# The second block's mixer in the order conv, q, k, pool, v, with its side work spread over the units

## The reference

```python
h = rms_norm(x, mix_norm[l])
u = h @ w_in[l]                       # 1024 -> conv 512, pool 256, q 512, k 512, v 512
y_conv = conformer_conv(...)          # a * sigmoid(gate), 31 taps over the tokens, layer norm, silu
y_pool = multiscale_pool(...)         # windows of 2, 4, 8, 16 tokens, then a 64 x 64 product per group
q = rms_norm(q.reshape(..., 4, 2, 64), q_norm[l]) * 64 ** -0.5
k = rms_norm(k.reshape(..., 4, 2, 64), k_norm[l])
...
a = p[:, :, 0] - lam * p[:, :, 1]     # p: softmax of q k^T - slope * distance, two maps per head
o = einsum(a, v)
y_attn = rms_norm(o, attn_subln[l]) * (1 - lambda_init)
x = x + concatenate([y_conv, y_pool, y_attn]) @ w_out[l]
```

## Time and profile before

| | |
|---|---|
| median of 3 runs | 2148.89 us (2148.51 to 2149.14) |
| the profiled execution | 2149.96 us, span 2148.1 us |
| PE busy in the span | 2097.4 us (98%) |
| DVE, ACT, POOL busy | 1253.8, 1091.8, 112.6 us |
| the two stages that the change touches | 1349.8 to 1463.9 us, 1838.0 to 1953.6 us |

### The profile page before, as it was taken

How to read it: one execution, slowest core, us unless ns; L and a number is a source line. 1 busy time by engine, 2 the same in 40 slices (tenths; PEclk the granted TensorE clock), 3 DMA queues, 4 the chain that set the end, 5 groups by cost and what they waited for, 6 DMA issues and landing times.

```text
span 2148.1 us, 24565 instructions
## 1 busy us (share of the span) xinstructions
PE 2097.4 (98%) x9840; PEld 1730.9 (81%) x9840; DVE 1253.8 (58%) x1609; ACT 1091.8 (51%) x1554; POOL 112.6 (5%) x128
## 2 busy tenths in 40 slices
PE   7999999999999999999999999979999999979998
PEld 6888788888888887888888888868888888868886
DVE  5555666555655556665556555676555555675554
ACT  5444564544554455554446444675444444665443
POOL 1000100000000000000000000140000000140000
PEclk9999999999999999999999999989999999989999
DMA  6554635555555554455556555525554655515553
GB/s 230 194 185 162 207 125 200 177 187 185 187 191 177 194 168 147 157 181 187 186 190 224 188 193 185 171 69 175 187 190 163 224 182 185 181 65 174 179 184 120
DMA packets 104545, 379.04 MB, mean 176 GB/s; under 512 B 11745, under 2 KB 11905, under 8 KB 104176
## 3 DMA queue, kind: packets, MB, share of 16 engines
q1 hardware_dynamic: 101808, 368.23, 51.6%
q0 software_dynamic: 2080, 8.21, 1.1%
q10 hardware_dynamic: 544, 1.05, 0.2%
HBM read 374.82 MB, written 2.62 MB: 176 GB/s over the span
## 4 chain that ended last, share of the span: by engine, by line
PE 86%; issue 9%; DVE 3%; ACT 2%; DMA 0%; POOL 0%; DVEq 0%; POOLq 0%; ACTq 0%
PE pb L333 26%; PE pb L335 26%; PE pb L334 25%; DVE scr L1297 2%; PE pb L389 2%; PE pb L352 1%; PE pb L375 1%; PE pb L427 1%; PE pb L373 1%; PE pb L374 1%; DVE wlo L1287 1%; ACT scr L1142 1%; PE pb L526 0%; ACT whi L866 0%; PE pb L500 0%
## 5 line engine op out<-in xcount | busy, mean ns | idle before, releaser
L1287 DVE TENSOR_TENSOR wlo<-raw,whi 128x1024 fp32r<-128x1024 f32 (+1 forms) x704 | 839.4, 1219 | 316.3 <-ACT whi L866 312.3
L866 ACT ACTIVATE whi<-raw 128x1024 fp32r<-128x1024 f32 (+1 forms) x704 | 716.3, 1050 | 212.3 <-PE pb L335 202.9
L333 PE MATMUL pb<-whi,XTh 128*128 128x512 f32 (+2 forms) x1904 | 751.3, 395 | 4.4 <-DVE wlo L1287 4.4
L335 PE MATMUL pb<-whi,XTl 128*128 128x512 f32 (+2 forms) x1904 | 737.6, 387 | 0.0
L334 PE MATMUL pb<-wlo,XTh 128*128 128x512 f32 (+2 forms) x1904 | 736.6, 387 | 0.0
L333 PEld LDWEIGHTS pb<-whi,XTh 128*128 128x128 f32 x1904 | 359.5, 189 | 79.6 <-DVE wlo L1287 5.9
L335 PEld LDWEIGHTS pb<-whi,XTl 128*128 128x128 f32 x1904 | 359.0, 189 | 74.3
L334 PEld LDWEIGHTS pb<-wlo,XTh 128*128 128x128 f32 x1904 | 359.7, 189 | 68.2
L333 PE MATMUL pb<-whi,HTh 128*128 128x512 f32 x816 | 321.5, 394 | 8.5 <-DVE HTl L1297 8.5
L335 PE MATMUL pb<-whi,HTl 128*128 128x512 f32 x816 | 319.2, 391 | 0.0
L334 PE MATMUL pb<-wlo,HTh 128*128 128x512 f32 x816 | 319.0, 391 | 0.0
(11 more groups left out here) (209 smaller groups left out, 1117.7 us busy)
## 6 DMA issues: line engine op xcount, KB each, us to landing
raw<-in_W SPq DMA_DIRECT2D x696, 512.0 KB, 4.2
raw<-in_W SPq DMA_DIRECT2D x8, 264.0 KB, 2.7
scratch<-scr POOLq DMA_DIRECT2D x1, 1536.0 KB, 6.4
scr<-in_bc POOLq DMA_DIRECT2D x2, 640.0 KB, 5.4
X<-in_x ACTq DMA_DIRECT2D x2, 512.0 KB, 9.1
scr<-scratch POOLq DMA_DIRECT2D x1, 1024.0 KB, 7.0
scr<-in_slope POOLq DMA_DIRECT2D x1, 1024.0 KB, 9.3
scr<-in_Pg POOLq DMA_DIRECT2D x1, 1024.0 KB, 12.5
```

The costliest lines, as they stand in the source:

```text
L333: pe.matmul(o, ah, bh, start=begin and i == 0, stop=False)
L335: ins = pe.matmul(o, al, bh, start=False, stop=end and done)
L866: return act.activation(o, i, ACT.Copy, scale=scale)
L1287: dve.tensor_tensor(wlo[u % W_SLOTS][:, 0:c], raw[u % RAW_SLOTS][:, 0:c], whi[u % W_SLOTS][:, 0:c].bitcast(F32), ALU.subtract).then_inc(*u ...
```

## The change

The 18 units of the input projection come in the order conv (k = 0 to 3), q (4 to 7), k (8 to 11), pool (12, 13), v (14 to 17), and the host lays the weights out so. The output projection takes its chunks as pool (2, 3), conv (0, 1), attention (4 to 7). The taps go by two lists, some at each k from 6 to 18, on ACT and DVE; POOL does the additions of taps 1 to 5, the root of q, taps 6 to 16, the root of k, taps 17 to 30. The batches that stood ahead of unit 18 on PE are spread over k = 15 to 22. The mean and variance of the conv norm come from `bn_stats` and `bn_aggr` on DVE, straight from PSUM, and DVE applies them, in place of two passes with sums and one to apply on ACT. `POOL_TAPS` is empty. In the core of the diff the lines that were removed from the loops are left out, since they stand in the functions above; the order of the hunks is PE, ACT, DVE, POOL, host.

```diff
-OUT2 = [2, 3, 4, 5, 6, 7, 0, 1]
+OUT2 = [2, 3, 0, 1, 4, 5, 6, 7]
...
+ACT_TAPS = [0, 3, 6, 9, 12, 15, 17, 19, 21, 23, 24, 26, 28, 31]
+DVE_TAPS = [0, 3, 6, 8, 11, 13, 16, 18, 21, 23, 25, 27, 29, 31]
...
+POOL_TAPS = range(31, 31)
+POOL_AT = (6, 17)
...
                     if k == 1:
                         rest(n)
...
+                    if k == 6:
+                        turn_pair(z, ("z", i, 1), "z", 4, ("zp", i))
+                    if k == 11:
+                        turn_head(q2, "q", 0, 5)
+                        turn_head(q2, "q", 1, 6)
                     if k == 15:
...
+                        turn_head(k2, "k", 0, 7)
+                        turn_head(k2, "k", 1, 4)
+                        pooled(0, 5)
+                        logits(0, 0, (6, 2))
+                        logits(0, 2, (3, 7))
+                        pooled(2, 4)
+                    if k == 16:
+                        pool_groups(4)
+                        logits(1, 0, (5, 6))
                     if k == 17:
...
+                        turn_pair(y[:, :, 256:512], ("pool_y", i), "pool", 7, ("pool_l", i, 1))
+                        logits(1, 2, (4, 3))
                     if k == 18:
...
+                        turn_maps(0, 0, 5)
+                        turn_maps(0, 2, 6)
                     if k == 19:
+                        values(0, 7)
                         turn_conv(4)
                     if k == 20:
...
+                        turn_maps(1, 0, 5)
+                        turn_maps(1, 2, 6)
+                        turn_pair(z, ("zn", i, 1), "zn", 4, ("conv_a", i, "yc", 1))
+                        values(1, 5)
+                    if k == 21:
+                        turn_y(0, 6)
                     if k == 22:
...
+                        turn_y(1, 7)
...
+                groups = [("z", 512, 2, 4), ("qn", 512, 2, 4), ("kn", 512, 2, 4), ("up", 256, 4, 2), ("v", 512, 2, 4)]
...
                 for k in range(18, 24):
...
                     if k == 3:
...
                         w.wait_ge(*at("r", n))
...
+                            w.wait_ge(*ended(u0 + 3, t))
                             act.activation(tmp[:, t, 0:256], pb[t][:, 256:512], ACT.Sigmoid,
...
+                    if k == 6:
                         w.wait_ge(*at("pair", i, "z"))
                         w.wait_ge(*at("z_pad"))
...
+                        copy(zp[:, :, 15:271], pb[4][:, :].rearrange("p (c t) -> p c t", c=2)).then_inc(*up("zp", i))
+                    if 6 <= k <= 18:
+                        tap_run(ACT_TAPS[k - 6], ACT_TAPS[k - 5])
+                    if k == 7:
+                        squares(7, 2, "q_sq2")
+                    if k == 11:
+                        w.wait_ge(*at("hcol"))
+                        turned("q", qT2, gq, 0, 5)
+                        turned("q", qT2, gq, 1, 6)
+                        squares(11, 0, "k_sq2")
...
+                            w.wait_ge(*ended(u0 + 13, t))
+                            scaled(up2[:, t, :], pb[2 + t][:, 0:256], n, t).then_inc(*up("up", i, t))
+                    if k == 15:
+                        turned("k", kT2, gk, 0, 7)
+                        turned("k", kT2, gk, 1, 4)
+                        pooled(0, 5)
+                        pooled(2, 4)
                         exps(0, (0, 4, 1, 5))
+                    if k == 16:
+                        w.wait_ge(*at("pool_p", i, "y"))
...
                         exps(0, (2, 6, 3, 7))
                     if k == 17:
+                        w.wait_ge(*at("pair", i, "pool"))
...
+                        exps(1, (0, 4))
...
+                            scaled(v2[:, t, :], pb[t][:, :], n, t).then_inc(*up("v", i, t))
                     if k == 18:
+                        turned_maps(0, 0, 5)
+                        turned_maps(0, 2, 6)
+                        exps(1, (1, 5, 2, 6, 3, 7))
                     if k == 19:
+                        value_squares(0, 7)
                     if k == 20:
+                        turned_maps(1, 0, 5)
+                        turned_maps(1, 2, 6)
                         w.wait_ge(*at("pair", i, "zn"))
...
+                        value_squares(1, 5)
+                    if k == 21:
+                        high_y(0, 6)
+                    if k == 22:
+                        high_y(1, 7)
...
+                    if k == 3:
...
+                    if 6 <= k <= 18:
+                        tap_run(DVE_TAPS[k - 6], DVE_TAPS[k - 5])
+                    if k == 8:
+                        head_mean("q")
+                    if k == 10:
+                        head_out("q", q2, 2)
+                    if k == 12:
+                        head_mean("k")
+                    if k == 14:
+                        head_out("k", k2, 0)
+                    if k == 15:
+                        maps(0, 0, (6, 2))
+                        maps(0, 2, (3, 7))
                         maps_max(0)
+                    if k == 16:
+                        maps(1, 0, (5, 6))
+                    if k == 17:
+                        w.wait_ge(*at("pool_h", i, 1))
...
+                        maps(1, 2, (4, 3))
                         maps_max(1)
                         maps_weights(0)
                         difference(0, 0)
                         difference(0, 2)
+                    if k == 18:
                         maps_weights(1)
                         difference(1, 0)
                         difference(1, 2)
+                    if k == 19:
...
+                        w.wait_ge(*at("pair", i, "acc"))
...
+                            dve.bn_stats(stats[:, 6 * t:6 * t + 6], pb[4][:, t * S:(t + 1) * S]).then_inc(
...
+                            dve.bn_aggr(mean_var[:, 2 * t:2 * t + 2], stats[:, 6 * t:6 * t + 6]).then_inc(
...
                         y_mean(0)
+                        w.wait_ge(*at("conv_r", i))
...
                     if k == 20:
+                        y_out(0, 7)
...
+                        y_mean(1)
+                    if k == 21:
+                        y_out(1, 5)
+                        low_y(0, 6)
+                    if k == 22:
+                        low_y(1, 7)
...
             def mixer2(s, i, n, m):
                 norm_root(n)
-                for name in ("q", "k"):
+                at_ = 1
+                for name, to in zip(("q", "k"), POOL_AT):
+                    add_taps(i, at_, to)
+                    at_ = to
                     root(col(i, "v_" + name, 16), col(i, "r_" + name, 16), 16, (name + "2_v", i, "v"), name + "2_r", i)
-                add_taps(i, 1, 25)
+                add_taps(i, at_, 31)
+                root(col(i, "v_conv", 2), col(i, "r_conv", 2), 2, ("conv_v", i, "v"), "conv_r", i)
                 root(col(i, "vy0", 4), col(i, "ry0", 4), 4, ("y_v", i, 0, "v"), "y_r", i, 0)
-                add_taps(i, 25, 31)
                 root(col(i, "vy1", 4), col(i, "ry1", 4), 4, ("y_v", i, 1, "v"), "y_r", i, 1)
-                root(col(i, "v_conv", 2), col(i, "r_conv", 2), 2, ("conv_v", i, "v"), "conv_r", i)
...
+        group(conv, 2)
         group(q, 2)
         group(k, 2)
-        group(conv, 2)
+        group(pool, 4)
         group(v, 2)
-        group(pool, 4)
         group(a["w_out_2"][i].reshape(KD, P, D)[OUT2].reshape(D, D), 1)
         ffn(a["ffn2_w_gate_2"][i], a["ffn2_w_up_2"][i], a["ffn2_w_down_2"][i])
```

## The result

The changed kernel takes 2163.1 us (median of 4 runs, 2162.59 to 2163.53) against 2148.74 us (4 runs, 2148.51 to 2149.14) for the kernel before beside it. The ratio is 1.0067, with a 95% interval of 1.0049 to 1.0084: slower, by 14.4 us.

A forecast was written before the change was run, and what follows sets the result against it. TensorE was taken as the bound. The walk gave 45.5 + 74.4 = 119.9 us per stage, with 2.5 us of low clock 122.4, together 15.1 us more over both stages: 2164 us on the median, range 2151 to 2172.

The forecast's parts named there:

- The first term: PE waits 8.9 us ahead of u11 for the q heads, where it waited nothing, plus 1.7 us of clock.
- E: The end of u11, put at 45.5 us from the stage's first unit; later times count from it.
- the ring: Four tap buffers: ACT's tap 10 waits for POOL's addition 6 behind q's root, so split 13 ends at 35.6.
- the rival of a ring that does not bind: Tap 10 gets its buffer in time; PE waits 3.6 us for the q heads; 2153 us; chance 0.08.
- Contention: POOL's additions slow DVE's split 13, two taps and q heads: 4.7 us in place of 3.6.
- The second term: PE waits 5.4 us at u14, ahead of the v units, for the k heads, plus 1.7 us of clock.
- The third term: PE, done with u17 at E + 34.0, waits 4.1 and 0.6 us for the first maps; before, 8.0.
- The fourth term: PE waits 3.95 us for the conv norm's normalised z, wanted at E + 48.3 and ready at E + 52.2.
- The low clock: PE at low clock after the waits for the maps and normalised z: 2.5 us added per stage, bounds 0 to 6.5.
- That the old norm "cost nothing": The conv norm's mean and square sum on ACT, now replaced, lay beside full PE work and cost nothing.
- The rival of only two waits: Maps and normalised z are never late, as DVE and ACT get ahead during PE's waits; 2142 us; chance 0.10.
- The clock rival: PE stays low after the map wait until the output units: 4 us more per stage, 2172 us; chance 0.16.

The follow-up runs named there:

- e1: Changed kernel with POOL's root of q moved behind the addition of tap 9 and its root of k behind that of tap 20: 2157.19 us.
- e6: Changed kernel with ACT's taps spread evenly and POOL's root of k behind the addition of tap 12: 2164.36 us.
- e7: Changed kernel with each tap addition on POOL 64 columns wide and not 256: 2161.95 us.
- e11: e10 with the edits of e9, ACT's taps spread evenly and POOL's root of k behind the addition of tap 14: 2141.49 us.
- e3: Changed kernel with DVE's means of the k heads ahead of split 15 and the k heads right behind split 16: 2151.94 us.
- e9: Changed kernel with ACT's exponential table loaded earlier and four DVE taps ahead of the low part of split 18: 2161.03 us.
- e8: Kernel before, with only the conv norm moved to statistics instructions on DVE: 2149.53 us, ratio 1.0001.
- e4: Changed kernel with the conv norm's sums and application back on ACT, without statistics instructions: 2169.10 us.
- e5: Changed kernel with all four head norm steps of q and k brought forward on DVE: 2144.61 us, ratio 0.9975.
- e10: e5 with k's squares ahead of the two q head copies on ACT and the y mean behind the normalised halves on DVE: 2148.07 us.
- e2: Changed kernel with the q heads' output on DVE ahead of split 13's low part: 2155.96 us.
- e12: e11 with the y mean moved back, k head steps and root of k earlier, and map work ahead of unit 21's split: 2135.78 us, ratio 0.9932.

## Why the prediction was right, and where its sizes were off

The forecast was 2164 us, and 2163.1 were measured; on the profiled execution 2165.1 against 2163.3. The chain of waits is the one that was forecast, but that the number fits so closely is luck in part: the two stages grew by 12.3 us and not by 15.1, and 1.1 us ahead of them, which nothing in the forecast stands for, hide some of the difference.

- **The first term held to 0.3 us.** With t from the stage's first unit (1350.91): root of q over at 32.5 (forecast 32.5), split 13 done at 35.7 (35.6), heads at 40.1 (40.3), E at 45.5 (1396.36; forecast 45.5). The wait is 8.64 us (8.9). That the ring holds the split is shown by e1 and e6, not only argued: without it the wait is 4.3 to 4.5 us, where the rival of a ring that does not bind had said 3.6 (its own numbers give 3.5).
- **Contention** was put at 1.1 us in that wait; e7 took 0.8 us of it away, with additions that were narrow and not gone. The rule of the Trainium skill (SBUF — State Buffer, Who interferes with whom), by which the loser of the shared ports is blocked for a whole instruction, would have had the three instructions lose some 2.5 us (an estimate). They lost 0.1, 0.4 and 0.4: on DVE's side the trace shows contention and not that price. On POOL's side it comes closer to the rule, as the last section shows. The longest that I found beside additions was a low part of a weight of 1.76 us in e11, against 1.22 alone.
- **The second term**: PE was at u14 at E + 5.9 (forecast 5.7), and it waited 5.28 us (5.4). e3 shows that it is the place of the head steps on DVE.
- **The third term was too large**: 2.96 and no second wait, against 4.1 and 0.6. DVE's side was right within 0.6 us (the first pair at E + 38.7 against 38.1). PE's was not: it had finished u17 at E + 35.8 and not at E + 34.0. The step that was off is "PE has finished u17 at E + 34.0": u15 ended 0.6 us later than in my walk, and from there to the end of u17 PE took 10.3 us where I had 9.1, since the 16 small matmuls of `pool_groups` alone took 1.6 us.
- **The fourth term's end was right and its wait too large.** Normalised z at E + 52.3 (forecast 52.2), with 0.38 us for a statistics instruction and 0.15 for an aggregation (0.4 and 0.2). PE wanted it at E + 50.2 and not at E + 48.3, as it was 1.9 us late by then, of which the low clock after the third wait, 1.7 us, is the larger part. So the wait is 2.1 us and not 3.95. The wait of 0.7 us at the conv chunks was not there (e1 and e3 had one of 0.8 and 1.0 us in layer 2).
- **The low clock**, 2.5 us added behind the walk, cost more by itself (1.7 us after each of the third and fourth waits, and 1.75 and 2.0 after the first two, where I had 1.7 each). But what came ahead of the fourth wait was paid out of that wait. This is why layer 2's stage is 121.1 us and not 122.4: the z that ACT and DVE make sets the time at E + 52.3, and low clock between the maps and it is free. e7 and e9 show it from the other side. The forecast also read the low clock of the kernel before too high: it took one stretch of about 9 and 13 us behind the long wait, at 4.5 and 6.5 us, where the trace has two, together 6.8 and 10.2 us long, that cost 3.1 and 4.8 us.
- In all, the waits grew by 5.5 and 5.4 us per stage and the low clock by 2.3 and 0.5 us (from 4.9 and 6.5 to 7.2 and 7.0). That makes 7.8 and 5.9 us, against 7.0 and 5.3 measured: this account is good to some 0.8 us.
- **That the old norm "cost nothing"** is right for the order of before (e8: ratio 1.0001) and wrong as a price for the new one. There the kernel without the statistics took 6 us more (e4), about half of it lost ahead of the norm.
- The rival of only two waits did not come: the third and fourth waits are there. That it named the right question is seen in e7 and e9: both waits hang on one list of ACT and DVE work, and how PE's time is shared between them does not move its end. The clock rival did not come either: the stretch behind the third wait was 3.4 us long in both layers.

What stays open is why the low stretch of the first wait was 6.8 us long in some stages and 10.2 us in others with the same wait of 8.6 us. It was 6.8 in both stages of after and 10.2 in both of e4, and 6.8 in layer 2 and 10.2 in layer 3 of e3 and e9. About half of what tells e4 from after goes with it, and no run here separates it.

## What to carry to other kernels

A strict engine list turns a small resource into a long wait: before you put work of one chain (taps) ahead of work of another (weight splits), follow its ring of buffers to the engine that frees it, and see what that engine does first. Price a wait of the bound engine by what comes back later: here the first wait gave a quarter (e1) to more than all (e6) of its savings back to the second. While the bound engine waits, the others catch up with their lists; take the wait away, and the next chain starts later (e3 against e5). And before moving an instruction off the path, look whether it stands in a gap that is there anyway: out of the root's shadow the y mean brought z 0.3 us sooner and cost 0.9 and 2.5 us behind it (e10 against e5).

## What the runs showed of the hardware that was not expected

- The granted clock fell 5.3 us after the start of the first wait (at 1387.70) and 2.5 us after the start of the second, and it fell behind the third and fourth waits only 0.35 and 0.4 us after PE had resumed. Low stretches were 3.4, 6.8 or 10.2 us long in the stages looked at, and 13.6 us at the 10.4 us wait of e6. Single waits of 0.9 to 1.5 us had no low stretch of their own, but in the kernel before one began at 1429.8 us, behind three waits of 0.9, 1.0 and 0.55 us. Of the waits of 1.8 to 2.5 us some had one (e5's fourth, 1.9 us; e2's first, 2.5 us, in layer 2) and some had none (e1's fourth, 1.9 us, in layer 2; e2's first in layer 3).
- A root on POOL that starts while DVE makes a low part takes longer by most of what is left of that instruction. The root of 128 x 4 took 1.00 us beside `tensor_scalar` on DVE and 1.91 us when it began 0.18 us into a low part (rows of after). The root of 128 x 16, which stands in both head chains, took 3.8 us in every head chain of before and after, since each began 0.17 us into a low part. In e12 (both layers) it took 2.91 us for q, where it began ahead of the low part, and 3.04 us for k, behind taps; the low part itself lost nothing beside it (1.23 us). So 0.8 to 0.9 us of each head chain are this. The forecast's 3.80 us has it in.

```profile
1447.85 1.00 POOL L1838 TENSOR_TENSOR st<-st,cst 128x4 f32<-128x4 f32 x1 [0.49 <-DVE st L1291]
...
1454.65 1.22 DVE L1270 TENSOR_TENSOR wlo<-raw,whi 128x1024 fp32r<-128x1024 f32 x1
1454.83 1.91 POOL L1838 TENSOR_TENSOR st<-st,cst 128x4 f32<-128x4 f32 x1 [5.97 <-DVE st L1291]
```

- An addition on POOL of 128 x 64 took 0.65 us (11 in 7.14) against 1.0 us for 128 x 256 (5 in 4.99): a quarter of the columns saved a third of the time.
- A table load on ACT of 1.28 us was followed at once by its exponential: in after, 1419.63 to 1420.92.
